# SwiGLU output products of three chunks in the seven-product form, with the gated rows as operands

## The chip, the cores and the metric

One core of one Trainium2 chip runs the whole step. The metric is the device time of one execution in microseconds; the kernel before has three runs, and the changed kernel is timed beside it.

## What is computed

One layer of a hybrid decoder on 544 tokens (512 of a prompt, 32 of eight sampled sequences), width 1024, float32. What the change touches is the feed-forward block, which stands in the layer twice, ahead of the token mixing and behind it:

```python
def swiglu(h, w_in, w_out):
    a, b = jnp.split(h @ w_in, 2, axis=-1)
    return (jax.nn.silu(a) * b) @ w_out

def run(x, ...):
    for l in range(DEPTH):
        x = x + 0.5 * swiglu(rmsnorm(x, norm_ffn1[l]), ffn1_w_in[l], ffn1_w_out[l])
        m, k, v, lf, s_fin = token_mix(rmsnorm(x, norm_mix[l]), w_in_mix[l], ...)
        x = x + m
        x = x + 0.5 * swiglu(rmsnorm(x, norm_ffn2[l]), ffn2_w_in[l], ffn2_w_out[l])
    return rmsnorm(x, norm_final), ...
```

`w_in` is 1024 by 5632, `w_out` is 2816 by 1024. The token mixing (projections, a gated linear recurrence and two forms of attention) is not touched.

## The kernel before, in words

Everything is kept with features on the 128 partitions and the 544 tokens in the free dimension, in two halves of 272. A float32 product is made of three passes: each operand is split into a rounded high part (`_hi`) and the rest (`_lo`), and high·high, high·low and low·high are summed in PSUM. ScalarE writes the high parts (a copy to float32r), VectorE the low parts (a subtraction).

The 2816 gate columns are 22 tiles of 128, worked in chunks of 4, 6, 6 and 6 (`CHUNKS`, L40). A chunk first makes its gate tiles (silu of one column tile times another), one **unit** for each, and then multiplies these rows into all 1024 output columns in four **out units** of 256 columns each, which are added to the residual `xT`. Units are numbered through the whole program; unit u uses weight slot u % 2, so that while TensorE works on one unit, ScalarE and VectorE split the weights of the next, and SyncE loads those of the one behind.

Chunk 0 and all out units are plain products (`products`, L2262): 3 passes for each tile of 128 rows, 128 columns and 272 tokens. Chunks 1 to 3 make their gate tiles by a seven-product form of a 2 by 2 block product (`seven_products`, L2391): the weights of a tile pair are four blocks of 128 by 512, `block_sums` and its relations (L2928 to L2971) form the sums `S1` to `S4` of them and the low parts, and the activations stand ready as seven operands `B11 ... T4`. So seven block products of 12 matmuls each take the place of eight. They go to five PSUM banks (`Z_BANKS`, L244), and VectorE joins them in five steps of 272 columns (L3008, L3013, L3018, L3022, L3026), with two bank copies (`z_kept`) by ScalarE (L2628, L2630). Then come the silu (L2607, L2635), the gated product (`z_gated`, L2973) and the split of the gated rows (`z_gated_hi`, L2609, and `z_gated_lo`, L2980).

There is no scheduler: each engine's order is written out in these functions, and an engine takes its instructions strictly in that order. VectorE's order for one gate unit is `seven_products_vector` (L2987): between the five steps of this unit stand the weight sums and the low parts of the next one. The out units are drained by `add_out` (L3028), two instructions of 544 columns that read PSUM and add half of it to `xT`. TensorE may begin a product only when its bank has been read; these waits are the `z_silu`, `z_step`, `z_copied` and `drained` waits at L2405 to L2440, and `g_wait` (L2461) holds an out unit until the gated rows are split. The slot waits of the loads are in `slot_free` (L2135).

The lines that the order of work hangs on, of a gate unit on VectorE:

```python
                if blocks:
                    block_sum_four(nxt, z + 1)
                    block_lo_gate(nxt, z + 1)
                else:
                    split_lo(nxt // 2, nxt % 2, last_kt)
                dve.wait_ge(z_product, 6 * z + 3)
                dve.wait_ge(z_copied, 2 * z + 1)
                nc.vector.tensor_tensor(z_part[:, 0, :], z_kept[:, 0, :], bank(beta), ALU.subtract).then_inc(z_step, 1)
                if blocks:
                    block_lo_sums(nxt, z + 1)
```

## Time and profile before

| | |
|---|---|
| median of 3 runs | 1224.8 us (1224.14 to 1225.08) |
| the profiled execution | 1225.52 us, of which its span is 1223.6 us |
| mean granted TensorE clock | 0.998 |
| TensorE, VectorE, ScalarE, GpSimdE busy | 98%, 72%, 48%, 8% of the span |
| DMA | 177.38 MB, 145 GB/s on average |

The span is what the trace shows of one execution. Busy shares are averages over stages: the two feed-forward blocks fill most of the span, the mixing the middle of it. A line number belongs to the kernel before. In a timeline the columns are the start, the duration, the engine, the line and the operation; in the table of windows they are the stretch and its length, each engine's busy time and number of instructions, the granted clock, and the DMA share and rate.

### The profile page before, as it was taken

How to read it: one execution, taken by the hardware profiler on the slowest of the kernel's cores; microseconds unless marked ns; L12 is line 12 of the kernel's file. 1: busy time of each engine (PE TensorE's matmuls, PEld its weight loads, DVE VectorE, ACT ScalarE, POOL GpSimd, SP SyncE). 2: the span in 40 equal slices, each digit the busy share in tenths (PEclk: the TensorE clock that was granted, in tenths of full speed). 3: DMA queues.
4: the chain of work that ended last, by engine and by line, in shares of the span. 5: the costliest groups of instructions: out<-in, count | busy, mean ns of one | idle time of the engine just before them, and what ended most of it. 6: DMA issues, size and time to landing. Idle time of an engine off the chain costs nothing.

```text
span 1223.6 us, 29870 instructions
## 1 busy us (share of the span) xinstructions
PE 1194.9 (98%) x11909; PEld 1115.8 (91%) x11909; DVE 882.9 (72%) x1661; ACT 586.7 (48%) x1101; POOL 102.4 (8%) x247
## 2 busy tenths in 40 slices
PE   9999999999999999998989999999999999999998
PEld 8999999999999999996656666699999999999998
DVE  6889848847959899746775676654889748838944
ACT  6354424524534344526867776634254424414534
POOL 1000000000013000000412522123000000000000
PEclk9999999999999999999999999999999999999999
DMA  8133333223334454376899997723133333233322
GB/s 212 53 87 103 113 95 101 89 89 103 96 100 153 129 132 104 104 241 201 307 351 351 367 363 247 254 78 97 53 91 102 110 95 104 87 102 88 96 78 74
DMA packets 195633, 177.38 MB, mean 145 GB/s; under 512 B 11921, under 2 KB 157874, under 8 KB 195250
## 3 DMA queue, kind: packets, MB, share of 16 engines
q1 hardware_dynamic: 194338, 171.93, 44.8%
q0 software_dynamic: 1104, 3.67, 0.8%
q8 instruction: 88, 1.44, 0.5%
q14 instruction: 39, 0.32, 0.1%
q10 hardware_dynamic: 64, 0.02, 0.0%
HBM read 164.42 MB, written 11.16 MB: 143 GB/s over the span
## 4 chain that ended last, share of the span: by engine, by line
PE 90%; DVE 3%; ACT 2%; issue 2%; DMA 2%; POOL 1%; ACTq 0%; DVEq 0%; POOLq 0%
PE ps L2400 38%; PE ps L2262 37%; PE ps L1071 2%; PE ps L1156 2%; PE ps L2492 2%; PE ps L1171 2%; PE ps L996 1%; PE ps L1036 1%; PE ps L1016 1%; DMA s_states<-in_state_hgrn 1%; DMA out<-s_states 1%; ACT d_keysT L1416 1%; PE ps L834 1%; PE ps L2508 0%; DMA gain_rows<-in_norm_final 0%
## 5 line engine op out<-in xcount | busy, mean ns | idle before, releaser
L2400 PE MATMUL ps<-b_lo,z_hi 128*128 128x272 f32 x1232 | 357.3, 290 | 0.0
L2400 PE MATMUL ps<-b_hi,z_lo 128*128 128x272 f32 x1008 | 290.6, 288 | 0.0
L2400 PE MATMUL ps<-b_hi,z_hi 128*128 128x272 f32 x1008 | 290.2, 288 | 0.0
L2400 PEld LDWEIGHTS ps<-b_lo,z_hi 128*128 128x128 f32 x1232 | 231.3, 188 | 0.0
L2400 PEld LDWEIGHTS ps<-b_hi,z_hi 128*128 128x128 f32 x1008 | 190.1, 189 | 0.0
L2400 PEld LDWEIGHTS ps<-b_hi,z_lo 128*128 128x128 f32 x1008 | 189.8, 188 | 0.0
L2557 ACT ACTIVATE w_hi<-w_raw 128x1536 fp32r<-128x1536 f32 (+2 forms) x48 | 74.7, 1556 | 161.8 <-PE ps L2262 161.8
L2262 PE MATMUL ps<-g_hi,w_hi 128*128 128x272 f32 x704 | 148.0, 289 | 0.3 <-DVE g_lo L2901 0.3
L2262 PE MATMUL ps<-g_lo,w_hi 128*128 128x272 f32 x704 | 147.5, 288 | 0.0
L2262 PE MATMUL ps<-g_hi,w_lo 128*128 128x272 f32 x704 | 146.8, 287 | 0.0
L3033 DVE SCALAR_TENSOR_TENSOR xT<-ps,xT 128x544 f32<-128x544 f32 x70 | 47.4, 719 | 97.9 <-PE ps L2262 97.9
L2956 DVE TENSOR_TENSOR z_lo<-z_sum,z_hi 128x1024 fp32r<-128x1024 f32 x132 | 113.6, 864 | 0.0
L2262 PEld LDWEIGHTS ps<-g_hi,w_hi 128*128 128x128 f32 x704 | 110.9, 188 | 0.8 <-DVE g_lo L2901 0.8
L2262 PEld LDWEIGHTS ps<-g_lo,w_hi 128*128 128x128 f32 x704 | 111.5, 189 | 0.0
L2262 PEld LDWEIGHTS ps<-g_hi,w_lo 128*128 128x128 f32 x704 | 111.2, 188 | 0.0
L2851 DVE TENSOR_TENSOR w_lo<-w_raw,w_hi 128x1536 fp32r<-128x1536 f32 (+2 forms) x47 | 89.7, 1908 | 15.2 <-ACT w_hi L2557 14.9
L2635 ACT ACTIVATE z_gate<-z_gate 128x272 f32<-128x272 f32 x36 | 15.5, 432 | 163.7 <-DVE z_gate L3026 163.7
L2956 DVE TENSOR_TENSOR z_lo<-w_raw,z_hi 128x1024 fp32r<-128x1024 f32 x88 | 83.8, 953 | 0.0
L1416 ACT ACTIVATE d_keysT<-ps 128x512 f32<-128x512 f32 x100 | 55.6, 594 | 52.4 <-PE ps L1071 52.1
L2585 ACT ACTIVATE z_hi<-w_raw 128x1024 fp32r<-128x1024 f32 x44 | 46.5, 1056 | 60.4 <-PE ps L2262 56.7
L1156 PE MATMUL ps<-d_keysT,d_queries 128*32 128x256 f32 x512 | 69.1, 389 | 1.4 <-issue 1.4
L2933 DVE TENSOR_TENSOR z_sum<-w_raw 128x1024 f32<-128x1024 f32 x44 | 53.8, 1223 | 22.0 <-PE ps L2400 17.7
(441 smaller groups left out, 2441.4 us busy)
## 6 DMA issues: line engine op xcount, KB each, us to landing
w_raw<-in_ffn_w_in SPq DMA_DIRECT2D x87, 512.0 KB, 5.0
d_keys<-in_cache_k SPq DMA_DIRECT2D x128, 256.0 KB, 5.3
...
w_raw<-in_w_in_mix SPq DMA_DIRECT2D x28, 512.0 KB, 4.8
...
w_raw<-in_w_out_mix SPq DMA_DIRECT2D x8, 512.0 KB, 4.6
...
```

Source lines behind the costliest of these rows:

```text
L1071: mm = pe.transpose(ps[:, B_KT + r, (k * SET_PAGES + m) * HP:(k * SET_PAGES + m + 1) * HP], d_k[n % K_RING][rows, m, j * P:(j + 1) * P], i ...
L1156: mm = pe.matmul(ps[g * NR:(g + 1) * NR, B_S, pp * 2 * PAGE:(pp + 1) * 2 * PAGE], d_q[b % 2][:, j * NR:(j + 1) * NR], keys, start=(j == 0) ...
L1171: pe.matmul(out, d_pT[b % 2][:, half, k, q * NR:(q + 1) * NR], src[:, q, :], start=(k == 0), stop=(k == 3), skip_group_check=True).then_in ...
L1416: nc.scalar.activation(d_kT[:, x % 2, k, :], ps[:, B_KT + k, :], ACT.Copy).then_inc(kc_act, 1)
L2262: mm = pe.matmul(bank(4 * j + 2 * t + half), wp, xp[:, k, half * HALF:(half + 1) * HALF], start=(k == 0 and wp is w[0] and xp is x_hi), st ...
L2400: mm = pe.matmul(bank(out), w[j][:, a, k * P:(k + 1) * P], x, start=(k == 0 and n_pass == 0 and not more), stop=(k == KB - 1 and n_pass == ...
L2557: nc.scalar.activation(w_hi[j][:, 0:kt * UC], w_raw[j][:, 0:kt * UC], ACT.Copy).then_inc(w_hi_ready, 1)
L2585: nc.scalar.activation(z_hi[j][:, A11:A12 + 1, :], z_raw[j][:, 0:2, :], ACT.Copy).then_inc(z_his, 1)
L2851: nc.vector.tensor_tensor(w_lo[j][:, 0:kt * UC], w_raw[j][:, 0:kt * UC], w_hi[j][:, 0:kt * UC].bitcast(F32), ALU.subtract).then_inc(w_lo_r ...
L2933: nc.vector.tensor_tensor(z_sum[j][:, S3:S1 + 1, :], z_raw[j][:, 0:4:3, :], z_raw[j][:, 2:3, :].to_broadcast([P, 2, BLOCK]), ALU.add).then ...
L2956: return nc.vector.tensor_tensor(z_lo[j][:, out, :], src, z_hi[j][:, out, :].bitcast(F32), ALU.subtract)
L3033: op = nc.vector.scalar_tensor_tensor(x, unit_psum(j, t), weight, x, ALU.mult, ALU.add)
```

## The change

The 22 gate tiles are worked in chunks of 4, 4, 4, 4 and 6. In chunks 1 to 3 (`BLOCKED`) the output product too is made by the seven-product form. The four gated tiles and the two token halves are the four blocks of one operand: the tiles 0 and 1 give `B11` and its neighbour, the tiles 2 and 3 give `B21` and `B22`. VectorE makes `T2`, `U1`, `T3` and `T4` of them, and seven operands are split in high and low, where four tiles were. They lie in rows of `g_full`, `g_high` and `g_low`. Such a chunk has two out units instead of four, each with 512 output columns: one load of weight blocks serves two results (v = 0 and 1), each a set of seven products of 6 matmuls. VectorE joins each result in the same five steps and adds it to `xT` in three instructions (`out_added`). A gated tile is no longer split by itself in these chunks. Chunk 0 and the last chunk keep the plain output product, and the counters of semaphores are renumbered.

```diff
 D_FF = 2816
 KD = D // P
 KF = D_FF // P
-CHUNKS = (4, 6, 6, 6)
+CHUNKS = (4, 4, 4, 4, 6)
+BLOCKED = (1, 2, 3)
...
+        g_full = [at(f"g{f + 1}_blocks", [P, 12, 2, HALF], F32, Z0 + 28 * (1 - f) * ROW) for f in range(2)]
+        g_low = [at(f"g{f + 1}_blocks_lo", [P, 6, 2, HALF], F32R, Z0 + 28 * (1 - f) * ROW) for f in range(2)]
+        g_high = [at(f"g{f + 1}_blocks_hi", [P, 6, 2, HALF], F32R, Z0 + (28 * (1 - f) + 6) * ROW) for f in range(2)]
...
+            def load_out_blocks(pair, j, w, k0):
+                slot_free(pair, j)
+                for r in range(2):
+                    dst = w_raw[j][:, r * 2 * BLOCK:(r + 1) * 2 * BLOCK].rearrange("p (k c) -> p k c", c=UC)
+                    src = w[0, k0 * P:(k0 + 4) * P, (2 * j + r) * UC:(2 * j + r + 1) * UC]
+                    sp.dma_start(dst, src.rearrange("(k p) n -> p k n", p=P)).then_inc(w_landed[j], 16)
...
+            def out_products(unit_n, j, z, f, c):
+                y = Y_AT[z]
+                def part(v, which, a, b, more=False):
+                    return product(j, Z_BANKS[v][which], a, (v, 2 + v), g_part_hi(f, b), g_part_lo(f, b), more)
+                def operand(b):
+                    if j == 0:
+                        pe.wait_ge(g_ready, g_from(f, c, G_LO) + TURN_ORDER.index(b) + 1)
+                pe.wait_ge(z_los, 4 * z + 2)
+                pe.wait_ge(w_lo_ready, unit_n)
+                pe.wait_ge(z_silu, 2 * (y - 1))
+                operand(B11)
+                part(0, 0, A11, B11).then_inc(z_product, 1)
+                pe.wait_ge(z_step, 5 * (y - 1))
+                operand(U1)
+                part(0, 1, S1, U1).then_inc(z_product, 1)
+                pe.wait_ge(z_silu, 2 * y)
+                part(1, 0, A11, B11).then_inc(z_product, 1)
+                pe.wait_ge(z_step, 5 * y)
+                part(1, 1, S1, U1).then_inc(z_product, 1)
+                pe.wait_ge(z_los, 4 * z + 3)
+                operand(T2)
+                part(0, 2, S2, T2).then_inc(z_product, 1)
+                operand(T3)
+                part(0, 3, S3, T3).then_inc(z_product, 1)
+                pe.wait_ge(z_los, 4 * z + 4)
+                operand(T4)
+                part(0, 4, A22, T4).then_inc(z_product, 1)
+                pe.wait_ge(w_lo_ready, unit_n + 1)
+                pe.wait_ge(z_copied, 2 * y + 2)
+                operand(B22)
+                part(0, 1, S4, B22, more=True).then_inc(z_product, 1)
+                operand(B21)
+                part(0, 0, A12, B21, more=True).then_inc(z_product, 1)
+                part(1, 2, S2, T2).then_inc(z_product, 1)
+                pe.wait_ge(z_step, 5 * y + 1)
+                part(1, 3, S3, T3).then_inc(z_product, 1)
+                pe.wait_ge(z_step, 5 * y + 2)
+                part(1, 4, A22, T4).then_inc(z_product, 1)
+                pe.wait_ge(z_copied, 2 * y + 4)
+                part(1, 1, S4, B22, more=True).then_inc(z_product, 1)
+                part(1, 0, A12, B21, more=True).then_inc(mm_done, 1)
...
+            def g_parts_hi(f, c, ns, gated):
+                act.wait_ge(gated_ready, g_from(f, c, GATED) + gated)
+                for n in ns:
+                    nc.scalar.activation(g_part_hi(f, n), g_part(f, T2 if n == U1 else n), ACT.Copy).then_inc(ghi_ready, 1)
+            def keep(y, bank_n, which, products):
+                act.wait_ge(z_product, products)
+                nc.scalar.activation(z_kept[:, which, :], bank(bank_n), ACT.Copy).then_inc(z_copied, 1)
...
+            def out_products_scalar(unit_n, z, f, c):
+                y, done = Y_AT[z], PRODUCTS_AT[z]
+                if unit_n % 2 == 0:
+                    z_silu_first(unit_n - 1, z - 1)
+                    g_parts_hi(f, c, TURN_ORDER[2:], 11)
+                act.wait_ge(z_step, 5 * (y - 1) + 3)
+                keep(y, Z_BANKS[0][0], 0, done + 1)
+                keep(y, Z_BANKS[0][1], 1, done + 2)
+                block_hi_raw(unit_n + 1, z + 1)
+                block_hi_raw_up(unit_n + 1, z + 1)
+                block_hi_sums(unit_n + 1, z + 1)
+                block_hi_last(unit_n + 1, z + 1)
+                act.wait_ge(z_step, 5 * y + 3)
+                keep(y + 1, Z_BANKS[1][0], 0, done + 3)
+                keep(y + 1, Z_BANKS[1][1], 1, done + 4)
...
+            def gated_place(f, c, tile):
+                if c not in BLOCKED:
+                    return z_up[:, :, :]
+                k = tile % 2
+                return g_full[f][:, B11:G_B12 + 1:G_B12 - B11, k, :] if tile < 2 else g_full[f][:, B21:B22 + 1, k, :]
+            def g_first_sum(f, c):
+                dve.wait_ge(gated_ready, g_from(f, c, GATED) + 2)
+                nc.vector.tensor_tensor(g_part(f, T2), g_part(f, B11), g_full[f][:, G_B12, :, :], ALU.subtract)\
+                    .then_inc(gated_ready, 1)
+            def g_sums(f, c, k):
+                done = g_from(f, c, GATED) + (4, 8)[k]
+                t2, b22 = g_part(f, T2)[:, k, :], g_part(f, B22)[:, k, :]
+                dve.wait_ge(gated_ready, done)
+                nc.vector.tensor_tensor(t2, t2, b22, ALU.add).then_inc(gated_ready, 1)
+                nc.vector.tensor_tensor(g_part(f, T3)[:, k, :], b22, g_full[f][:, G_B12, k, :], ALU.subtract)\
+                    .then_inc(gated_ready, 1)
+                dve.wait_ge(gated_ready, done + 1)
+                nc.vector.tensor_tensor(g_part(f, T4)[:, k, :], t2, g_part(f, B21)[:, k, :], ALU.subtract)\
+                    .then_inc(gated_ready, 1)
+            def g_parts_lo(f, c, ns):
+                for n in ns:
+                    dve.wait_ge(ghi_ready, g_from(f, c, G_HI) + TURN_ORDER.index(n) + 1)
+                    nc.vector.tensor_tensor(g_part_lo(f, n), g_part(f, T2 if n == U1 else n),
+                                            g_part_hi(f, n).bitcast(F32), ALU.subtract).then_inc(g_ready, 1)
...
+            def out_added(unit_n, y, v):
+                j = unit_n % 2
+                lower, upper = halves(xT[:, 4 * j + 2 + v, :]), halves(xT[:, 4 * j + v, :])
+                dve.wait_ge(z_step, 5 * y + 5)
+                nc.vector.scalar_tensor_tensor(lower, z_up[:, :, :], 0.5, lower, ALU.mult, ALU.add)
+                nc.vector.scalar_tensor_tensor(upper[:, 1, :], z_gate[:, 1, :], -0.5, upper[:, 1, :], ALU.mult, ALU.add)
+                if v:
+                    dve.wait_ge(mm_done, unit_n + 1)
+                nc.vector.scalar_tensor_tensor(upper[:, 0, :], bank(Z_BANKS[v][0]), -0.5, upper[:, 0, :], ALU.mult, ALU.add)\
+                    .then_inc(z_silu, 2)
+                if v:
+                    dve.wait_ge(z_silu, 2 * y + 2)
+                    dve.sem_inc(drained, 1)
+            def out_products_vector(unit_n, z, f, c, before):
+                y, done = Y_AT[z], PRODUCTS_AT[z]
+                nxt = unit_n + 1
+                before()
+                block_sums(nxt, z + 1)
+                block_sum_two(nxt, z + 1)
+                block_sum_four(nxt, z + 1)
+                block_lo_gate(nxt, z + 1)
+                alpha, gamma, beta, delta, eps = Z_BANKS[0]
+                first_part(y, beta, done + 5)
+                second_part(y, delta, done + 6)
+                lower_right(y)
+                block_lo_sums(nxt, z + 1)
+                lower_left(y, eps, done + 7)
+                upper_right(y, gamma, done + 8)
+                block_lo_two(nxt, z + 1)
+                dve.wait_ge(z_product, done + 9)
+                out_added(unit_n, y, 0)
+                block_lo_up(nxt, z + 1)
+                alpha, gamma, beta, delta, eps = Z_BANKS[1]
+                first_part(y + 1, beta, done + 10)
+                second_part(y + 1, delta, done + 11)
+                lower_right(y + 1)
+                lower_left(y + 1, eps, done + 12)
+                block_lo_four(nxt, z + 1)
+                upper_right(y + 1, gamma, done + 13)
...
+                        if c in BLOCKED:
+                            p0 += pairs
+                            def g_last(c=c, z=z0 + kt):
+                                z_gated(z - 1, gated_place(f, c, 3))
+                                g_sums(f, c, 1)
+                                g_parts_lo(f, c, TURN_ORDER[2:])
+                            out_products_vector(2 * p0, z0 + kt, f, c, g_last)
+                            out_products_vector(2 * p0 + 1, z0 + kt + 1, f, c,
+                                                lambda: out_added(2 * p0, Y_AT[z0 + kt] + 1, 1))
+                            def before(unit_n=2 * p0 + 1, y=Y_AT[z0 + kt + 1] + 1):
+                                out_added(unit_n, y, 1)
+                            p0 += 1
+                            continue
```

The helpers `first_part`, `second_part`, `lower_right`, `lower_left` and `upper_right` are the five steps that stood in `seven_products_vector`, and `keep` is the bank copy of ScalarE. In a gate unit of a blocked chunk `z_gated_lo` is gone; the third one has `g_first_sum` and the low parts of `B11` and `U1`, the fourth `g_sums`.

**VectorE behind the last gate tile of chunk 1 and in its first out units, before** (`z_gate`, `z_part`, `z_up`, `z_kept` are parts of a result, `g_hi` and `g_lo` the high and low part of a gated tile, `w_raw`, `w_hi` and `w_lo` those of weights):

```order
L3026 TENSOR_TENSOR z_gate<-z_part,ps 128x272 [waits z_product]
L2978 TENSOR_TENSOR z_up<-z_gate,z_up 128x544 [waits z_silu,z_step]
L2984 SCALAR_TENSOR_TENSOR g_lo<-z_up,g_hi 128x544 [waits ghi_ready]
L2851 TENSOR_TENSOR w_lo_85<-w_raw_81,w_hi_83 128x1536 [waits w_hi_ready]
L3033 SCALAR_TENSOR_TENSOR xT<-ps,xT 128x544 [waits mm_done]
L3033 SCALAR_TENSOR_TENSOR xT<-ps,xT 128x544
L2851 TENSOR_TENSOR w_lo_84<-w_raw_80,w_hi_82 128x1536 [waits w_hi_ready]
L3033 SCALAR_TENSOR_TENSOR xT<-ps,xT 128x544 [waits mm_done]
L3033 SCALAR_TENSOR_TENSOR xT<-ps,xT 128x544
```

**The same engine behind the last gate tile of chunk 1, now** (`g_blocks` holds the seven operands, `g_block` the last of them; `z_sum`, `z_hi` and `z_lo` are sums, high and low parts of weight blocks):

```order
L3180 TENSOR_TENSOR z_gate<-z_part,ps 128x272 [waits z_product]
L3118 TENSOR_TENSOR g_blocks<-z_gate,z_up 128x2x272 [waits z_silu,z_step]
L3145 TENSOR_TENSOR g_blocks<-g_blocks 128x272 [waits gated_ready]
L3146 TENSOR_TENSOR g_blocks<-g_blocks 128x272
L3149 TENSOR_TENSOR g_block_128<-g_blocks 128x272 [waits gated_ready]
L3156 TENSOR_TENSOR g_blocks_lo<-g_blocks,g_blocks_hi 128x544 [waits ghi_ready] x2
L3156 TENSOR_TENSOR g_block_lo<-g_block_128,g_block_hi 128x544 [waits ghi_ready]
L3156 TENSOR_TENSOR g_blocks_lo<-g_blocks,g_blocks_hi 128x544 [waits ghi_ready] x2
L3072 TENSOR_TENSOR z_sum_91<-w_raw_81 128x1024 [waits mm_done,w_landed1]
L3078 TENSOR_TENSOR z_sum_91<-w_raw_81,z_sum_91 128x512 [waits z_sums]
L3084 TENSOR_TENSOR z_sum_91<-w_raw_81,z_sum_91 128x512 [waits z_sums]
L3095 TENSOR_TENSOR z_lo_89<-w_raw_81,z_hi_87 128x1024 [waits z_his]
```

Between the last gate tile and the drain of the first out unit stood a gated product, one low part and a weight split. Now there are the gated product, three sums, five low parts and the whole set of weight sums, and the first joining step comes behind all of these.

**VectorE in the first out unit of chunk 1, further on, now:**

```order
L3095 TENSOR_TENSOR z_lo_89<-z_sum_91,z_hi_87 128x512 [waits z_his]
L3228 SCALAR_TENSOR_TENSOR xT<-z_up,xT 128x544 [waits z_step,z_product]
L3229 SCALAR_TENSOR_TENSOR xT<-z_gate,xT 128x272
L3232 SCALAR_TENSOR_TENSOR xT<-ps,xT 128x272
L3095 TENSOR_TENSOR z_lo_89<-w_raw_81,z_hi_87 128x512 [waits z_his]
L3162 TENSOR_TENSOR z_part<-z_kept,ps 128x272 [waits z_copied,z_product]
L3167 TENSOR_TENSOR z_part<-z_part,ps 128x272 [waits z_step,z_product]
L3172 TENSOR_TENSOR z_up<-z_part,z_kept 128x272 [waits z_step,z_copied]
L3176 TENSOR_TENSOR z_up<-z_part,ps 128x272 [waits z_product]
L3095 TENSOR_TENSOR z_lo_89<-z_sum_91,z_hi_87 128x512 [waits w_hi_ready]
L3180 TENSOR_TENSOR z_gate<-z_part,ps 128x272 [waits z_product]
L3228 SCALAR_TENSOR_TENSOR xT<-z_up,xT 128x544 [waits z_step]
```

Before, an out unit was two drains and a weight split. Now the three additions of the first result stand in front of the five steps of the second result, and the additions of the second behind those.

## Rows read from the trace of the kernel before

**Rows 1.** The page: busy time of two engines, and TensorE's granted clock in 40 slices
```profile
PE 1194.9 (98%) x11909; PEld 1115.8 (91%) x11909; DVE 882.9 (72%) x1661; ACT 586.7 (48%) x1101; POOL 102.4 (8%) x247
PEclk9999999999999999999999999999999999999999
```
**Rows 2.** The chain that ended last, chunks 1 and 2: start, length, what
```profile
89.70 63.57 PE ps L2400 x504
153.27 36.07 PE ps L2262 x288
189.34 63.57 PE ps L2400 x504
252.91 36.07 PE ps L2262 x288
```
**Rows 3.** Windows: one gate unit of chunk 2
```profile
210.53:221.12 10.59, 10.59 (x87) 10.59 (x86) 9.61 (x15) 5.51 (x10) 0.00 (x0) 1.00 0.37 101
```
**Rows 4.** Timeline of VectorE, the same kind of unit
```profile
200.05 1.23 DVE L2933 TENSOR_TENSOR z_sum<-w_raw 128x1024 f32<-128x1024 f32 x1 [0.97 <-PE ps L2400]
201.20 0.72 DVE L2978 TENSOR_TENSOR z_up<-z_gate,z_up 128x544 f32<-128x544 f32 x1
201.83 0.69 DVE L2939 TENSOR_TENSOR z_sum<-w_raw,z_sum 128x512 f32<-128x512 f32 x1
202.64 0.72 DVE L2984 SCALAR_TENSOR_TENSOR g_lo<-z_up,g_hi 128x544 fp32r<-128x544 f32 x1
203.28 0.68 DVE L2945 TENSOR_TENSOR z_sum<-w_raw,z_sum 128x512 f32<-128x512 f32 x1
203.88 1.22 DVE L2956 TENSOR_TENSOR z_lo<-w_raw,z_hi 128x1024 fp32r<-128x1024 f32 x1
205.02 0.43 DVE L3008 TENSOR_TENSOR z_part<-z_kept,ps 128x272 f32<-128x272 f32 x1
205.37 1.22 DVE L2956 TENSOR_TENSOR z_lo<-z_sum,z_hi 128x1024 fp32r<-128x1024 f32 x1
206.50 0.43 DVE L3013 TENSOR_TENSOR z_part<-z_part,ps 128x272 f32<-128x272 f32 x1
...
209.35 0.43 DVE L3026 TENSOR_TENSOR z_gate<-z_part,ps 128x272 f32<-128x272 f32 x1
```
**Rows 5.** Timeline of ScalarE, the same unit
```profile
201.95 0.66 ACT L2612 ACTIVATE g_hi<-z_up 128x544 fp32r<-128x544 f32 x1 [0.61 <-DVE z_up L2978]
202.51 0.62 ACT L2589 ACTIVATE z_hi<-w_raw 128x512 fp32r<-128x512 f32 x1
203.03 0.38 ACT L2628 ACTIVATE z_kept<-ps 128x272 f32<-128x272 f32 x1
203.31 0.39 ACT L2630 ACTIVATE z_kept<-ps 128x272 f32<-128x272 f32 x1
```
**Rows 6.** Timeline, two engines, behind the fifth gate tile of chunk 2
```profile
242.36 0.40 ACT L2607 ACTIVATE z_gate<-ps 128x272 f32<-128x272 f32 x1 [0.32 <-PE ps L2400]
...
242.93 0.72 DVE L2978 TENSOR_TENSOR z_up<-z_gate,z_up 128x544 f32<-128x544 f32 x1 [1.36 <-ACT z_gate L2607]
```
**Rows 7.** Timeline: TensorE held by a low part of VectorE, first out unit
```profile
69.10 0.73 DVE L2901 TENSOR_TENSOR g_lo<-ffn_gated,g_hi 128x544 fp32r<-128x544 f32 x1 [0.72 <-ACT g_hi L2578]
...
69.89 0.52 PE L2262 MATMUL ps<-g_hi,w_hi 128*128 128x272 f32 x2 [0.17 <-DVE g_lo L2901]
```
**Rows 8.** Windows at the head of the mixing, behind the last projection
```profile
553.00:556.00 3.00, 1.38 (x47) 0.94 (x49) 3.00 (x4) 2.00 (x5) 2.43 (x7) 1.00 0.56 168
556.00:560.00 4.00, 4.00 (x102) 2.86 (x88) 1.13 (x7) 2.34 (x4) 0.00 (x0) 0.57 0.88 268
560.00:564.00 4.00, 4.00 (x95) 2.47 (x82) 3.70 (x18) 1.98 (x4) 0.00 (x0) 1.00 0.27 77
```
**Rows 9.** The page: loads of gate weights, KB each, us from issue to landing
```profile
w_raw<-in_ffn_w_in SPq DMA_DIRECT2D x87, 512.0 KB, 5.0
```

265 lines of the change are left out of this document (163 added, 102 removed).

## The prediction

> **What bounds the kernel now.** I began with the page's first line [rows 1]: TensorE is busy 98% of the span and its granted clock never leaves the upper level, 2.4 GHz. A busy TensorE can still be a waiting one, so I took the chain of waits next [rows 2]: chunk 1 is one piece of 504 matmuls in 63.57 us and one of 288 in 36.07 us, and chunk 2 follows without a gap. That is 126.1 ns for a matmul of a seven-product unit and 125.2 ns for one of a plain out unit, with nothing between them. TensorE is the only bound in the feed-forward blocks, and a matmul left out there is worth its full 126 ns as long as nothing else comes to hold it.
>
> The next question is how near the second engine is. In one gate unit of 10.59 us VectorE is busy 9.61 us [rows 3]. The 72% of the page is an average over stages; here it is 91%, and the timeline shows the rest as one wait of 0.97 us at the unit's head [rows 4]. ScalarE, at 5.51 us, is far from its limit.
>
> **The change part by part.** *TensorE.* A tile of gated rows costs 288 / 6 = 48 matmuls in the plain out units. Twelve tiles of a feed-forward block move to the new form: 576 matmuls of 125.2 ns, 72.1 us, go; three chunks with 2 x 84 = 168 matmuls of 126.1 ns, 63.6 us, come. The gate units are as many as before. That saves 8.6 us a block, **17.1 us** in all, if TensorE never waits. Smaller groups (6 matmuls instead of 12) cost nothing by themselves, since the pitch is that of single matmuls.
>
> *VectorE.* From one start to the next in the timeline, 272 columns take 0.35 us, 512 take 0.60, 544 take 0.635 and 1024 take 1.14 [rows 4]. The weight sums and low parts of a unit are three instructions of 1024 and five of 512, 6.4 us; the five joining steps are 1.75. The new shapes (three additions of 544, 272 and 272 to `xT`, sums of 272, low parts of 544) are in no row. I bound them by the pitch, 0.35 and 0.635, and by the full duration of one instruction, 0.43 and 0.72 [rows 4], and take the pitch, since the nearest rows have the same operands and follow each other so. A blocked chunk then holds six weight sets (38.4), four times five steps in the gate units and four times five in the out units (14.0), four gated products (2.5), a sum of 544 and six of 272 (2.7), seven low parts (4.4), and four times three additions of 1.34 (5.3): **67.4 us of VectorE in a chunk of 6 x 10.6 = 63.6 us of TensorE**. The gate units have room (8.8 us of 10.6 without `z_gated_lo`), the two out units have 13 to 16 us of work in 10.6 each, and since only one unit is prepared ahead, room in one place does not help in the other.
>
> *Where TensorE waits.* I follow the order of the change through the two out units, counting from the first one's start; TensorE's products are 6 x 0.126 = 0.76 us each.
> - The gated product of tile 3 needs ScalarE's two silus. In the row it starts 0.6 us behind the unit [rows 6]; here VectorE, which has 10.7 us of work in the third gate unit and 9.9 in the fourth, ends its last step only at 0.1, and the second silu comes behind that, so 0.9. Then the gated product and three sums end at 2.8. ScalarE writes five high parts at 0.56 each [rows 5] from 2.85, VectorE the low parts from 3.55 at 0.635. Low part `T2` is done at 4.3; TensorE has made its four products of `B11` and `U1` by 3.0 and waits **1.3**. The later operands keep ahead of it.
> - VectorE is through with the low parts at 6.7, then come the four instructions of the next unit's sums, to 10.4, and only then `first_part`, done at 10.9. TensorE's eleventh product writes the bank which that step reads, and could start at 8.85: **2.1**, and 0.15 for the late bank copies.
> - TensorE ends the unit at 14.1. The next one starts in the bank of the first result. Its last addition stands behind `block_lo_sums`, two steps and `block_lo_two`, and is done at 15.7: **1.6**.
> - After two products it wants the bank of the second result, and the order there is `block_lo_up`, five steps, `block_lo_four` in between, and three additions: 20.35 instead of 17.2, **3.15**.
> - From there TensorE has 12 products, 9.1 us, and VectorE keeps up. The unit ends at 29.4 instead of 21.2. The next gate unit starts with VectorE 3 us late; its waits reach back to what is done by then, and VectorE gains 1.8 us in a unit, so nothing more is lost.
>
> This is 8.3 us a blocked chunk, six times: 49.6 us. An instruction that waits for two semaphores starts up to 0.1 later than one with a single wait (0.17 in [rows 6] against 0.03 from product to high part in [rows 4, 5]); the steps that follow each other directly pay it, 0.25 us a chunk on the path, 1.5 in all. TensorE itself restarts 0.06 behind its releaser [rows 7], which is in the above. Moved otherwise, and free: the loads. Two per out unit of 512 KB land in 5.0 us [rows 9], with a whole unit of time behind the issue; if VectorE is late, they are issued late by as much, but then VectorE is what is waited for. ScalarE's seven high parts for four (3 x 0.56 a chunk) are covered by its idle half.
>
> *The clock.* One place of the trace shows it falling. At the head of the mixing TensorE was busy 1.38 of 3 us, and in the 4 us behind that the mean granted clock was 0.57, before it was 1.00 again [rows 8]: (1 - 0.57) / 0.5 of 4 us are some 3.4 us at the lower level, 1.2 GHz, worth 1.7 us. The Trainium skill (TensorE: Matmul & The Clock Gate, Part 1) says that the slow clock is the default and activity is what releases it; by this rule the change could pay for its waits a second time, and the trace agrees. The second out unit has such a place: from 14.1 to 20.35 TensorE works 1.5 of 6.3 us. I take a fall in three of the six chunks, 3 x 1.7 = 5 us; none and all six are the bounds, 0 and 10.
>
> **Sum.** 1225.5 - 17.1 + 49.6 + 1.5 + 5 = 1264.5 us against the profiled execution, which lies 0.7 us above the median: **1264 us**.
>
> **Rivals.** *The saving arrives (faster).* VectorE stays hidden, and the time is 1225 - 17 = 1208. The Trainium skill (Perfetto Trace Analysis, Identifying the Most-Contended Engine) says to improve the engine with the highest occupancy, and that is TensorE, from whose list the change strikes 144 matmuls. By that rule alone it is 1208. For it: two chunks in a row without a wait of TensorE [rows 2]. Against it: 67.4 us of VectorE do not fit in 63.6, whatever their order. It decides where the waits of a chunk stay under 17.1 / 6 = 2.85 us; the two out units would have to lose 5 us of VectorE work. Chance 0.05.
>
> *Only the surplus counts.* The order leaks less than I walked, and TensorE loses just 67.4 - 63.6 = 3.8 us a chunk: 1225 - 17 + 23 = 1231. Against it: four different products wait at four places, and the work in front of each is fixed by the order. Chance 0.10.
>
> *The clock falls everywhere or the new instructions take their full duration.* The first gives 1269. By the second some 28 new instructions of a chunk cost 0.085 more, 2.4 us and 14 in all, if all lie on the path: 1273 to 1278. Chance 0.15.
>
> **Numbers.** The forecast has 0.70, with 1255 to 1270 as its own range (hand-offs of 0.02 to 0.08 us, clock 0 to 10). To hold eight in ten of all cases the range reaches a little into both neighbours: 1246 to 1277. A measurement of this kernel tells 0.2%, 2.5 us, from no change. Faster 0.05, same 0.02, slower 0.93.
>
> **What would show it.** In the trace after, TensorE's waits should stand in the lines of the products with `g_hi` operands, 8 us a blocked chunk at four or five places, the longest near 3 us and released by an addition to `xT`; gate units should still take 10.6 us, a blocked chunk 71 to 74 us, and the last chunk be unchanged. A granted clock below 1 in second out units shows the last term. I am wrong if the out units take 10.6 us each (then 1208), if VectorE has idle time of more than 2 us in them while TensorE waits (then a wait on ScalarE or a load is what I missed), or if gate units grow.

## The result, and the profile after

| | before | after |
|---|---|---|
| median of the runs | 1224.8 us | 1272.8 us (1270.6 to 1274.8, 3 runs) |
| ratio | | 1.0388 [1.0363, 1.0413]: slower |
| profiled execution, span | 1225.5, 1223.6 us | 1270.6, 1268.7 us |
| mean granted clock | 0.998 | 0.986 |

The forecast was 1264 us with a range of 1246 to 1277. The page of after, the lines that answer to [rows 1] and [rows 9], and its chain:

```profile
PE 1197.7 (94%) x11765; PEld 1112.2 (88%) x11765; DVE 1017.3 (80%) x1961; ACT 631.1 (50%) x1211; POOL 102.1 (8%) x247
PEclk9999999998999999999999999999999998999999
...
PE 65%; DVE 23%; issue 7%; ACT 3%; DMA 1%; POOL 1%; DVEq 0%; ACTq 0%; POOLq 0%
...
w_raw<-in_ffn_w_out SPq DMA_DIRECT2D x24, 512.0 KB, 4.4
```

The 144 matmuls are gone (11909 - 11765), yet TensorE's busy time has not shrunk: matmuls are longer at the lower clock and behind a wait (0.36 to 0.39 us instead of 0.29 for the first one, in the rows below). A quarter of the chain is now VectorE (23%). The new loads land in 4.4 us and are waited for nowhere.

TensorE's waits, the list of after (engine, instruction held, releaser, then us in total, times, longest); before, no seven-product matmul waited for VectorE:

```profile
PE ps L2441 <- DVE xT L3232: 22.0, 10, 3.0
PE ps L2441 <- DVE z_part L3162: 10.6, 6, 1.8
PE ps L2441 <- DVE g_blocks_lo L3156: 8.3, 6, 1.8
```

TensorE's timeline in chunk 2 (start, duration, instruction, and in brackets the idle time before it):

```profile
210.65 0.36 PE L2441 MATMUL ps<-g_blocks_hi,z_hi 128*128 128x272 f32 x1 [1.08 <-DVE g_blocks_lo L3156]
...
217.18 0.39 PE L2441 MATMUL ps<-g_blocks_hi,z_hi 128*128 128x272 f32 x1 [1.76 <-DVE z_part L3162]
...
226.82 0.39 PE L2441 MATMUL ps<-g_blocks_hi,z_hi 128*128 128x272 f32 x1 [2.96 <-DVE xT L3232]
```

These three are the low part of `T2`, `first_part` before the eleventh product, and the second result's addition to `xT`, in the order of the walk. The fourth, at the start of the second out unit, is only 0.3 to 0.4 us here, since the clock had fallen at 218.4 and TensorE was late itself. By the starts of the matmuls in chunk 3 of the second block, where it did not fall before the last of them, the four are 1.25, 1.93, 1.54 and 3.12 us, where the walk had 1.3, 2.1, 1.6 and 3.15. In the first chunk of each block the first wait is longer, 2.0 us, with 0.6 more ahead of it.

VectorE is the other half of the picture. Windows of after: the four gate units of chunk 2, then one whole blocked chunk, from the first product of its out units to that of the next chunk's (columns as in [rows 3]: PE, PEld, DVE, ACT, POOL, the clock, the DMA share and rate):

```profile
157.30:167.90 10.60, 10.60 (x86) 10.60 (x85) 9.86 (x20) 3.26 (x7) 0.00 (x0) 1.00 0.04 11
167.90:178.50 10.60, 10.60 (x86) 10.60 (x85) 10.41 (x18) 4.30 (x8) 0.00 (x0) 1.00 0.43 118
178.50:189.00 10.50, 10.50 (x86) 10.50 (x85) 10.04 (x16) 4.47 (x9) 0.00 (x0) 1.00 0.55 173
189.00:199.40 10.40, 10.40 (x85) 10.40 (x84) 10.40 (x19) 6.74 (x15) 0.00 (x0) 1.00 0.20 58
206.38:278.59 72.21, 66.26 (x506) 65.22 (x505) 69.24 (x118) 33.34 (x61) 0.00 (x0) 0.98 0.30 88
```

TensorE is never idle in the gate units, but VectorE is busy there for 9.9 to 10.4 us of 10.6 too, and for 69.2 of the 72.2 us of the chunk.

**Where the time went.** The feed-forward blocks hold six blocked chunks. From the first to the last matmul with `g_blocks` operands, the two out units take 32.5, 29.6, 31.4, 32.8, 31.1 and 31.0 us: 188.4, against 6 x 21.2 = 127.1 without waits. Less the 17.1 saved, that is +44.2. The mixing adds 1.1: it begins behind a last run of plain products that has moved by 21.2 us (401.73 to 422.89), and before the second block the like has moved by 22.3 (852.89 to 875.16). Together 45.3, where the span has grown by 45.1 us. The mixing's 1.1 need not be a price of the change: this stretch is the same in all kernels here and lasts between 449.2 and 457.8 us in their profiled executions, 451.0 before.

Of the 188.4, 6.4 belong to the clock: the same six intervals take 182.0 us in the kernel with fillers below, where the clock does not fall in them. The gate units behind them give 1.4 back, so the two blocks as wholes differ by 5.0 us. The clock fell at eight places of the feed-forward blocks, five times behind the longest wait of a chunk and three times behind the wait of the eleventh product; one of the five:

```profile
299.70:304.00 4.30, 4.30 (x24) 4.30 (x24) 3.86 (x5) 2.10 (x3) 0.00 (x0) 0.60 0.72 201
```

### The profile page after: what moved, and what is told of

Read it like the earlier page. It is cut to its first block, busy times and chain, and to the rows that moved or that the text cites. A ratio compares the mean times of both kernels' runs of the same rounds, so it can differ in the third digit from the quotient of the medians.

```text
span 1268.7 us, 30008 instructions
## 1 busy us (share of the span) xinstructions
PE 1197.7 (94%) x11765; PEld 1112.2 (88%) x11765; DVE 1017.3 (80%) x1961; ACT 631.1 (50%) x1211; POOL 102.1 (8%) x247
## 4 chain that ended last, share of the span: by engine, by line
PE 65%; DVE 23%; issue 7%; ACT 3%; DMA 1%; POOL 1%; DVEq 0%; ACTq 0%; POOLq 0%
PE ps L2441 27%; PE ps L2309 23%; DVE z_lo L3095 6%; PE ps L1104 2%; PE ps L1189 2%; PE ps L2593 2%; DVE z_sum L3072 2%; DVE g_blocks_lo L3156 2%; PE ps L1204 2%; PE ps L1029 1%; DVE z_sum L3078 1%; DVE g_blocks L3118 1%; DVE z_part L3167 1%; DVE z_up L3172 1%; PE ps L1069 1%
## 5 line engine op out<-in xcount | busy, mean ns | idle before, releaser
L3095 DVE TENSOR_TENSOR z_lo<-z_sum,z_hi 128x1024 fp32r<-128x1024 f32 x168 | 144.5, 861 | 0.0
L2441 PE MATMUL ps<-g_blocks_hi,z_hi 128*128 128x272 f32 x288 | 90.7, 315 | 42.3 <-DVE xT L3232 22.0
L2658 ACT ACTIVATE w_hi<-w_raw 128x2048 fp32r<-128x2048 f32 (+2 forms) x32 | 50.9, 1591 | 104.7 <-PE ps L2309 104.7
L2441 PEld LDWEIGHTS ps<-g_blocks_hi,z_hi 128*128 128x128 f32 x288 | 59.0, 205 | 48.3 <-DVE xT L3232 19.1
L2441 PE MATMUL ps<-g_blocks_lo,z_hi 128*128 128x272 f32 x288 | 87.7, 304 | 0.0
L2441 PE MATMUL ps<-g_blocks_hi,z_lo 128*128 128x272 f32 x288 | 87.7, 304 | 0.0
L2724 ACT ACTIVATE z_kept<-ps 128x272 f32<-128x272 f32 x120 | 42.0, 390 | 66.0 <-DVE z_up L3172 56.1
L2990 DVE TENSOR_TENSOR w_lo<-w_raw,w_hi 128x2048 fp32r<-128x2048 f32 (+2 forms) x31 | 61.6, 1986 | 13.4 <-ACT w_hi L2658 13.1
L1189 PE MATMUL ps<-d_keysT,d_queries 128*32 128x256 f32 x512 | 69.4, 391 | 0.0
L2309 PE MATMUL ps<-g_hi,w_hi 128*128 128x272 f32 x320 | 68.5, 289 | 0.3 <-DVE g_lo L3040 0.3
L2309 PE MATMUL ps<-g_lo,w_hi 128*128 128x272 f32 x320 | 68.1, 288 | 0.0
```

The source lines that it names most:

```text
L1189: mm = pe.matmul(ps[g * NR:(g + 1) * NR, B_S, pp * 2 * PAGE:(pp + 1) * 2 * PAGE], d_q[b % 2][:, j * NR:(j + 1) * NR], keys, start=(j == 0) ...
L2309: mm = pe.matmul(bank(4 * j + 2 * t + half), wp, xp[:, k, half * HALF:(half + 1) * HALF], start=(k == 0 and wp is w[0] and xp is x_hi), st ...
L2441: mm = pe.matmul(bank(out), w[j][:, a, column * P:(column + 1) * P], x[:, k, :], start=(k == 0 and n_pass == 0 and not more), stop=(k == l ...
L2658: nc.scalar.activation(w_hi[j][:, 0:kt * UC], w_raw[j][:, 0:kt * UC], ACT.Copy).then_inc(w_hi_ready, 1)
L2724: nc.scalar.activation(z_kept[:, which, :], bank(bank_n), ACT.Copy).then_inc(z_copied, 1)
L2990: nc.vector.tensor_tensor(w_lo[j][:, 0:kt * UC], w_raw[j][:, 0:kt * UC], w_hi[j][:, 0:kt * UC].bitcast(F32), ALU.subtract).then_inc(w_lo_r ...
```

## The experiments

The theory on record was that four products of a blocked chunk wait for VectorE, which has more to do in the two out units than TensorE, and that the clock's falls come on top. The rivals were that the small chunks cost by themselves, that lateness builds up over chunks, that one wait in one order is to blame, and, later, that the whole list of VectorE is the bound and no place in it. Each kernel is compared with the kernel before on the same chip (1223.5, 1225.0, 1225.6 and 1224.5 us in the four lots, in order: 1 to 4, 5 to 8, 9 and 10, 11 and 12).

### 1. The chunks alone

```diff
-BLOCKED = (1, 2, 3)
+BLOCKED = ()
...
```

> Chunks of 4, 4, 4, 4 and 6, all output products plain. If the seven-product output form is what costs time, this is the kernel before again: the same matmuls (22 tiles of 48 in each block), one more change from gate to out units, 1224.8 us within 2. If the smaller chunks themselves cost something (rival: more changes of stage, less room ahead of the out units), a good part of the 48 us is seen here.

Measured 1227.0 us, ratio 1.0029 [1.0015, 1.0043]. No seven-product matmul is on TensorE's list of waits, and the plain chunks start 66.4 us apart. Of the 1.4 us that its span is longer, 0.75 stand in the mixing, where the clock fell twice. The form costs the time, not the chunks.

### 2. One blocked chunk of three

```diff
-BLOCKED = (1, 2, 3)
+BLOCKED = (3,)
...
```

> Only chunk 3 has the seven-product output form; chunks 1 and 2 have plain out units. If each blocked chunk costs its own share (its waits, 7 to 9 us, and about one fall of the clock, 1.7 us, against 2.85 us of matmuls saved), two chunks instead of six cost a third of 48 us: 1241, between 1237 and 1244. If the loss builds up from chunk to chunk (rival: VectorE's lateness is carried on), it is clearly less than a third, under 1236.

Measured 1242.8 us, ratio 1.0146 [1.0129, 1.0163]: 18 us for two blocked chunks, 9 each, where the change has 48 / 6 = 8. Its out units take 31.1 and 31.0 us, as in the change. The trace puts it closer: the two feed-forward blocks are 7.2 and 7.0 us longer than before, against 7.1 and 7.6 a blocked chunk in the change, and the mixing, which is unchanged, happened to take 6.8 us more in this execution. So each chunk pays its own price, and nothing builds up.

### 3. Matmuls in the waits

```diff
+            def fill(n, b=4):
+                for _ in range(n):
+                    pe.matmul(ps[:, b, 0:P], ones[:, :], ones[:, :], start=True, stop=True)
...
+                if j:
+                    pe.wait_ge(z_step, 5 * (y - 1))
+                    fill(5)
...
+                if j:
+                    fill(12)
...
+                if j == 0:
+                    fill(4)
...
+                if j == 0:
+                    fill(7, 6)
```

> The changed kernel with matmuls of ones (4, 7, 5 and 12 of 128 columns, about 0.23 us each) placed ahead of the four long waits of each blocked chunk, so that TensorE stays active in them. If the clock falls because of the waits, and costs what the trace of the changed kernel shows (8 falls in the two blocks, 1.7 us each), this gives 1272.8 - 13 = about 1260, with a granted clock near 0.998. If the waits alone are the cost and the low clock falls into time that is waited anyway (rival), the time stays at 1271 to 1274 though the clock is full; if the fillers outlast the waits it is slower.

Measured 1264.2 us, ratio 1.0332 [1.0317, 1.0346]; clock 1.0. That is 0.0056 or 7 us less than the change (less than I expected). In the profiled executions 5.0 us of it lie in the feed-forward blocks, and that is the price of the clock there; the rest lies in the mixing, where the clock fell twice in the change and not here. The out units take 182.0 us in all. A chunk of it, windows:

```profile
205.41:277.91 72.50, 71.31 (x562) 70.11 (x561) 69.38 (x119) 33.50 (x61) 0.00 (x0) 1.00 0.30 88
```

With TensorE busy for 71.3 us the chunk still lasts 72.5, and VectorE's busy time is unchanged. The chunk of the change above, 72.21 us, is not shorter: counted on VectorE, from the gated product of tile 3 to that of the next chunk, it is 72.48 us in the change (207.16 to 279.64) and 72.50 here, with the same 118 instructions at the same distances.

### 4. The joining steps ahead of the weight sums

In the first out unit `first_part`, `second_part` and `lower_right` stand before the sums of the next weights, so that the eleventh product is not held.

```diff
                 before()
...
+                if unit_n % 2 == 0:
+                    first_steps()
                 block_sums(nxt, z + 1)
...
```

> In the first out unit VectorE makes the first three joining steps ahead of the weight sums of the next unit. The wait of 1.9 us ahead of TensorE's eleventh product loses its releaser. If each wait is worth its own length (rival), six times 1.9 us go: 1261. If VectorE's whole list of the chunk sets the time, the order inside it doesn't matter: the wait ahead of the eleventh product is gone, those ahead of the bank copies and at the second out unit's start grow by as much, and the time is 1272.8 within 3.

Measured 1273.6 us, ratio 1.0409 [1.0391, 1.0426]: nothing gained. The wait for `z_part` left the list, and its time came back under two others (compare the list of after):

```profile
PE ps L2441 <- DVE xT L3232: 27.5, 12, 3.0
PE ps L2441 <- ACT z_kept L2724: 5.8, 4, 1.5
```

### 5. Less work in the out units

On the kernel with fillers (4, 7, 2 and 8 of them) the first two of the three additions of each result to `xT` are left out.

```diff
-                nc.vector.scalar_tensor_tensor(lower, z_up[:, :, :], 0.5, lower, ALU.mult, ALU.add)
-                nc.vector.scalar_tensor_tensor(upper[:, 1, :], z_gate[:, 1, :], -0.5, upper[:, 1, :], ALU.mult, ALU.add)
```

> On the kernel with filled waits (1264.2 us, full clock; fillers cut to 4, 7, 2 and 8). Left out: the first two of the three additions of each result to xT in the blocked chunks, so three quarters of their output never reach the residual. That takes 1.0 us of VectorE four times a chunk. If VectorE's list sets the time of a blocked chunk, 2 us a chunk go at least (two of the four stand ahead of the last long wait), up to 3.9 if all four count: 1240 to 1252. If the waits are set by the hand-offs between the engines and not by its load (rival), less than 1 us a chunk: above 1258.

Measured 1253.6 us, ratio 1.0240 [1.0222, 1.0257]: 11 us or 1.9 a chunk less than with all additions. Windows of one chunk:

```profile
203.21:273.27 70.06, 69.37 (x548) 68.51 (x547) 65.62 (x110) 33.72 (x62) 0.00 (x0) 1.00 0.31 91
```

VectorE lost 3.8 us of busy time and the chunk 2.4. (The two blocks are 14.2 us shorter, 2.4 a chunk; the ratio shows less, since the mixing took 4.1 us more in this execution.) TensorE, with its fillers, is busy for 69.4 of 70.1 us here and so nearly full itself. So the run bounds the gain from below.

### 6 and 7. One more low part, in a gate unit or in an out unit

The prediction said that the gate units have room which is of no use to the out units. If so, an extra instruction of 1024 columns is free in the one and not in the other. Both write a low part a second time, on the kernel with fillers.

```diff
+                    if c in BLOCKED and n == 1:
+                        block_lo_again(nxt, z + 1)
```

> On the kernel with filled waits (1264.2): one instruction of 1024 elements (a low part written twice) more for VectorE in the second gate unit of each blocked chunk, 1.14 us, six in all. As the prediction has it, VectorE gains 1.8 us in such a unit and room there is of no use elsewhere: 1264 to 1266. If instead VectorE's list of the whole chunk, gate units too, sets its length (rival), about 1.0 us a chunk: 1270 to 1271.

```diff
                 block_sum_two(nxt, z + 1)
+                if unit_n % 2 == 0:
+                    block_lo_again(nxt, z + 1)
```

> On the kernel with filled waits (1264.2): the same instruction more in the first out unit of each blocked chunk instead. Both theories have it on the path, 1.14 us six times: 1271. If it is hidden (hand-offs set the waits), 1264 to 1265.

Measured 1269.1 us, ratio 1.0360 [1.0345, 1.0375], and 1269.5 us, ratio 1.0366 [1.0350, 1.0383]. One chunk of each, windows, the gate unit's first:

```profile
208.96:282.48 73.52, 71.57 (x563) 70.15 (x561) 70.44 (x120) 33.47 (x61) 0.00 (x0) 1.00 0.30 87
```

and the out unit's:

```profile
206.47:279.98 73.51, 71.30 (x562) 70.10 (x561) 70.43 (x120) 33.56 (x61) 0.00 (x0) 1.00 0.29 87
```

The chunk is 1.0 us longer in both, 73.52 and 73.51 against 72.50, for 1.05 us more of VectorE. It makes no difference where the instruction stands. (The ratios say 0.6 to 0.7 us a chunk with some 0.4 of uncertainty; the traces, 1.0 in every chunk. It is not the 1.14 of a pitch, since at either place the instruction parts two sums of which the second takes the first's result, which saves 0.12.) There is no room in the gate units that is not already used.

### 8. The sums S2 and S4 on GpSimd

In the blocked chunks GpSimd makes the two additions of 512 columns of each weight set. In the second out unit TensorE makes the upper products first, so that the bank of the second result is wanted late, ScalarE copies the banks before the last high parts, and 8 fillers a chunk stay.

```diff
+                    nc.gpsimd.tensor_tensor(z_sum[j][:, S2, :], z_raw[j][:, 0, :], z_sum[j][:, S1, :], ALU.add).then_inc(z_sums, 1)
...
+                    nc.gpsimd.tensor_tensor(z_sum[j][:, S4, :], z_raw[j][:, 1, :], z_sum[j][:, S2, :], ALU.add).then_inc(z_sums, 1)
```

> A try for a faster version, with filled waits: in the blocked chunks GpSimd makes the two weight sums of 512 (some 2.1 us each, by its row of 544 elements), TensorE finishes the first result of the second out unit before it begins the second, and ScalarE makes the bank copies of the second result ahead of the last high parts. If VectorE's load is the bound, 1.2 us a unit leave its list and a blocked chunk goes from 72.5 to about 69 us: 1264 - 20 = 1244, still above the kernel before. If GpSimd's reads slow VectorE or its sums come late (rival), it is 1255 or more.

Measured 1279.0 us, ratio 1.0450 [1.0431, 1.0469]: the slowest of all, 35 us over what I expected. Windows of a chunk:

```profile
206.84:282.76 75.92, 70.20 (x522) 68.66 (x521) 72.84 (x110) 33.69 (x61) 20.54 (x12) 0.96 0.29 84
```

Two groups of instructions on each engine, VectorE's of 146 us with chunks 2 and 3, GpSimd's of the whole span (shapes, count, then busy us, mean ns of one, and idle time before):

```profile
L3135 DVE TENSOR_TENSOR z_lo<-z_sum,z_hi 128x1024 fp32r<-128x1024 f32 x12 | 20.4, 1701 | 0.0
L3135 DVE TENSOR_TENSOR z_lo<-w_raw,z_hi 128x1024 fp32r<-128x1024 f32 x12 | 19.9, 1662 | 0.3
...
L3656 POOL TENSOR_TENSOR z_sum<-w_raw,z_sum 128x512 f32<-128x512 f32 x36 | 66.6, 1850 | 463.0 <-DVE z_sum L3112 463.0
L3658 POOL TENSOR_TENSOR z_sum<-w_raw,z_sum 128x512 f32<-128x512 f32 x36 | 57.4, 1595 | 2.8
```

VectorE has twelve sums less and is busy for 72.8 us instead of 69.4. Its waits in this chunk are for ScalarE, 0.9 and 0.7 us, as without GpSimd; it waits nowhere for a sum that comes late. Its low parts of 1024 columns take 1.7 us on average, where they take 1.22 in [rows 4]. The timeline of both engines shows one of them:

```profile
220.18 2.31 DVE L3135 TENSOR_TENSOR z_lo<-z_sum,z_hi 128x1024 fp32r<-128x1024 f32 x1
...
217.76 2.20 POOL L3656 TENSOR_TENSOR z_sum<-w_raw,z_sum 128x512 f32<-128x512 f32 x1 [14.51 <-DVE z_sum L3112]
220.04 1.37 POOL L3658 TENSOR_TENSOR z_sum<-w_raw,z_sum 128x512 f32<-128x512 f32 x1
```

GpSimd started at 220.04, VectorE at 220.18; GpSimd ended at 221.41, VectorE 1.08 us after that, near the 1.22 that such an instruction takes alone. The first GpSimd instruction was long in the same way, behind a low part of VectorE that ended at 218.82. They go one after the other. VectorE's joining steps that read PSUM, at 218.74 and 219.27, took their usual 0.43 and 0.44 us beside the same GpSimd instruction. The Trainium skill (SBUF — State Buffer, SBUF: two separate sides) says that the two engines share a pair of ports, that whichever starts first holds it for its whole instruction, when VectorE reads two inputs from SBUF, and that the other is blocked. The trace agrees: 2.31 us is 1.23 of blocking and one low part.

### 9. The same kernel without the work of the sums

```diff
-                    nc.gpsimd.tensor_tensor(z_sum[j][:, S2, :], z_raw[j][:, 0, :], z_sum[j][:, S1, :], ALU.add).then_inc(z_sums, 1)
+                    nc.gpsimd.tensor_tensor(z_sum[j][:, S2, 0:16], z_raw[j][:, 0, 0:16], z_sum[j][:, S1, 0:16], ALU.add).then_inc(z_sums, 1)
```

> The kernel with the sums on GpSimd, but GpSimd's two additions a unit in the blocked chunks are made over 16 of their 512 columns alone, and the parts of S2 and S4 are taken of the raw blocks A11 and A12 (the second products of the blocked chunks are then not the reference's). All waits, the order of the products and the order of the VectorE steps stay as in the kernel with the sums on GpSimd, which took 1279.0 us. Theory 1 (GpSimd and VectorE slow each other: in that kernel the 1024-column low parts took 1.66 to 1.70 us where they take 1.22 alone, and GpSimd's 512-column additions 1.60 to 1.85): VectorE's list of a blocked chunk is 67.4 - 8 x 0.69 = 61.9 us, under TensorE's 63.6 and its 2.7 of fillers, and the chunks fall from some 75.5 us to 67 to 69: 1228 to 1240 us. Theory 2 (the loss lies in the waits and in the order of the products, or in the high parts that come after the copies on ScalarE): at most 10 us are gained, 1268 us or more.

Measured 1243.2 us, ratio 1.0151 [1.0132, 1.0171]; a chunk, window:

```profile
200.82:270.12 69.30, 67.00 (x522) 65.73 (x521) 62.53 (x106) 33.57 (x61) 7.75 (x12) 1.00 0.32 92
```

37 us come back, so the loss of kernel 8 was the work on GpSimd and not its order: theory 1, though 3 us above its range. VectorE's list has the same shapes in the same order as in kernel 8, and it is busy for 62.5 us instead of 72.8: 10.3 us of a chunk were stretch. (A part of the 37 is the clock, which fell six times in the blocks of kernel 8 and never in those of this one; by kernel 3 that is a few us.) The expectation counts 8 sums in a chunk; there are twelve, two for each of six weight sets. The chunk is now 6.8 us longer than VectorE's busy time. Something else begins to hold it: VectorE waits for TensorE for 2.3 us of this chunk, which it did not do in kernel 8.

### 10. The order of kernel 8, all sums on VectorE

```diff
+                if j:
...
+                    part(0, 0, A12, B21, more=True).then_inc(z_product, 1)
+                    pe.wait_ge(z_silu, 2 * y)
+                    part(1, 0, A11, B11).then_inc(z_product, 1)
```

> The kernel with the sums on GpSimd, but with all sums back on VectorE, at the places that they have in the change: what stays of it is the order of TensorE's products in the second out unit (the upper half first, so that the bank of the second result is wanted late), the copies of the banks ahead of the last high parts, and 8 filler matmuls a chunk. Theory 1 (a blocked chunk lasts as long as VectorE's list of 67.4 us and some 5 us in which VectorE waits, whatever TensorE's order): near the kernel with fillers alone (1264 us), 1258 to 1268 us. Theory 2 (the places of the waits decide, and this order hides two of the three of the second out unit, 3.1 and 1.5 us a chunk less 1 of filler): 1242 to 1252 us. Theory 3 (this order is what cost the kernel with the sums on GpSimd its time): 1275 us or more.

Measured 1265.8 us, ratio 1.0326 [1.0310, 1.0343]. A chunk (window), and under it TensorE's waits in the span:

```profile
205.13:277.62 72.49, 67.24 (x523) 65.75 (x521) 69.37 (x119) 33.48 (x61) 0.00 (x0) 1.00 0.30 88
```
```profile
PE ps L2441 <- DVE z_part L3202: 16.8, 12, 1.8
PE ps L2441 <- DVE xT L3272: 8.9, 10, 1.4
PE ps L2441 <- DVE g_blocks_lo L3196: 4.5, 6, 1.1
```

This is the run that decides. The waits stand at other products, with other lengths, 20 fewer filler matmuls run, and the chunk is 72.49 us against 72.50. VectorE's chain, with its waits for ScalarE, gives this number. I summed it from its timeline in this chunk: the start-to-start times of its 118 instructions by shape (0.35, 0.60, 0.635 and 1.14, as in [rows 4]; the windows count 119, with one that lies across an edge) make 67.6 us; waits for ScalarE, at the gated product of tile 3 and at the low part behind it, make 1.8; and the rest is 3.1. Of this, 2.5 is in pairs where an instruction waits for the VectorE instruction just before it, nearly always for its result, and 0.5 in the two sums that come right behind the last addition of a result to `xT`, where `drained` is raised. The same sum in kernel 3, and in chunk 2 of the change itself, gives the same numbers. Such pairs in the timeline of after:

```profile
226.99 1.23 DVE L3072 TENSOR_TENSOR z_sum<-w_raw 128x1024 f32<-128x1024 f32 x1 [0.21 <-DVE xT L3232]
228.25 0.69 DVE L3078 TENSOR_TENSOR z_sum<-w_raw,z_sum 128x512 f32<-128x512 f32 x1
228.97 0.69 DVE L3084 TENSOR_TENSOR z_sum<-w_raw,z_sum 128x512 f32<-128x512 f32 x1
229.58 1.22 DVE L3095 TENSOR_TENSOR z_lo<-w_raw,z_hi 128x1024 fp32r<-128x1024 f32 x1
230.72 0.43 DVE L3162 TENSOR_TENSOR z_part<-z_kept,ps 128x272 f32<-128x272 f32 x1
231.25 0.44 DVE L3167 TENSOR_TENSOR z_part<-z_part,ps 128x272 f32<-128x272 f32 x1
231.79 0.44 DVE L3172 TENSOR_TENSOR z_up<-z_part,z_kept 128x272 f32<-128x272 f32 x1
```

From 230.72 to 231.25 it is 0.53 us, where the same step gives way to an independent one in 0.35 (205.02 to 205.37 in [rows 4]); a sum of 512 behind a sum takes 0.72 instead of 0.60. In the gate units most of these steps have other work between them; in the out units they stand together.

### 11. Dependent steps apart

```diff
                 first_part(y + 1, beta, done + 10)
+                block_lo_up(nxt, z + 1)
                 second_part(y + 1, delta, done + 11)
+                block_lo_four(nxt, z + 1)
                 lower_right(y + 1)
...
+                    block_lo_gate(nxt, z + 1)
                     block_sum_four(nxt, z + 1)
-                    block_lo_gate(nxt, z + 1)
```

> The kernel with the upper products first, and on VectorE no step straight behind the step whose result it takes, where another is at hand: the first low part between the sums, a sum or a low part between the joining steps. Nothing is left out. Theory 1 (VectorE's own chain is the whole chunk: in a blocked chunk of 72.49 us of that kernel, 67.6 us are the start-to-start times of its 119 instructions, 3.1 the extra 0.1 to 0.19 us of a step that waits for the VectorE instruction just before it, 1.8 waits for ScalarE): some 12 of those pairs go, 1.7 to 2 us a chunk, 10 to 12 us: 1253 to 1257 us. Theory 2 (the extra is hidden by something else that sets the end, a load or ScalarE): unchanged, 1263 us or more.

Measured 1261.8 us, ratio 1.0309 [1.0291, 1.0327]. Neither theory's number: the change to kernel 10 is 0.0017, 2 us, with the intervals overlapping, though the trace is plain (72.03 us a chunk instead of 72.49). By the same sum of VectorE's timeline most of the pairs are gone, 2.2 us, and new waits of 1.8 have come. VectorE's waits in one chunk:

```profile
DVE z_lo L3135 <- ACT z_hi L2738: 1.3, 2, 0.6
DVE g_blocks L3158 <- ACT z_gate L2746: 1.0, 1, 1.0
DVE g_blocks_lo L3196 <- ACT g_blocks_hi L2757: 0.7, 1, 0.7
```

The first line is new: the low part of `S2` was brought forward, and ScalarE's high part of it is not there yet. Most of the gain was given back to it.

### 12. Without the sums and without fillers

```diff
-                    fill(5)
...
-                fill(3)
...
                 first_part(y + 1, beta, done + 10)
+                block_lo_up(nxt, z + 1)
                 second_part(y + 1, delta, done + 11)
```

> The kernel with the sums left out (GpSimd's additions over 16 columns alone, the parts of S2 and S4 of the raw blocks, so the second products of the blocked chunks are not the reference's), without the 8 filler matmuls a chunk and with the joining steps of the out units apart from each other. It tells what the form is worth where VectorE has 6.9 us less in a chunk. Theory 1 (then TensorE is the bound, 63.6 us and 1 to 2.2 us of waits): chunks of 64.8 to 66 us against 66.4 before, 1216 to 1224 us, as fast as the kernel before or faster. Theory 2 (what the order costs TensorE stays, and the clock falls in its waits): 67 to 69 us a chunk, 1228 to 1240 us.

Measured 1247.1 us, ratio 1.0183 [1.0166, 1.0200]; a chunk (window), and under it TensorE's waits in the span:

```profile
201.57:271.64 70.07, 65.28 (x506) 63.82 (x505) 62.18 (x106) 33.80 (x61) 8.03 (x12) 1.00 0.32 91
```
```profile
PE ps L2441 <- DVE xT L3278: 12.0, 12, 1.0
PE ps L2441 <- ACT z_kept L2760: 8.4, 12, 1.0
PE ps L2441 <- DVE g_blocks_lo L3195: 6.5, 6, 1.1
```

Theory 1 fell, and even theory 2 was too hopeful. With 6.9 us less of VectorE work the form is still slower than the plain chunk of 66.4 us, and no engine is full: TensorE's list is 63.6 of 70.1, VectorE's busy time 62.2. Now they wait for each other, and for ScalarE's bank copies: in this chunk VectorE waits for TensorE for 2.7 us and for ScalarE for 4.2. (In the profiled execution the mixing took 4.6 us more than before; the blocks alone are 3.6 us a blocked chunk longer.) So behind the bound that the change meets stands a second one at about 69 to 70 us, a chain of hand-offs through three engines. Which link of it is the tightest stays open.

None of the twelve beats the kernel before. One with all its work would have to bring a blocked chunk from 72.5 to under 66.4 us, and the start-to-start times of VectorE alone are 67.6.

## Why the prediction was right, and where it was not

- **TensorE's saving**: 144 matmuls fewer, as counted; kernel 1 shows that nothing else of the regrouping costs more than 0.3%.
- **The waits of a blocked chunk**: 49.6 and 1.5 us were forecast, 51.1. At full clock (kernel 3) the two blocks are 39.0 us longer than before; with the 17.1 saved that makes 56.1. All four places are in the trace within 0.2 us of the walk, in its order, and the sign against them did not show: while TensorE waits in a chunk, VectorE is idle for 0.5 to 1.4 us, not for more than 2. Of the 5.0 us more, 2.7 are in the first chunk of each block. There the gated product of tile 3 starts 2.2 us behind the first product instead of 1.1, and the out units take 1.2 to 1.5 us longer; I take it that VectorE comes late out of the plain chunk, which no run tested. The rest is 0.4 us a chunk of hand-offs.
- **The term that was too small** is VectorE's list of 67.4 us with 0.25 for dependent steps. The pitches were right (its terms, unrounded, make 67.6, and so do the traces), the hand-offs are 3.1 us and the waits for ScalarE 1.8. The walk had the latter.
- **The clock**: 5 us forecast, from three falls of 1.7. The 5.0 measured agree by luck: there were eight falls in these blocks, and they cost less each. The three behind the eleventh product's wait cost nothing (a chunk with one such fall has VectorE's full-clock length, 72.48 us), since the slower matmuls lie in time that is waited anyway; the five behind the longest wait cost 0.9 to 1.0 us each (73.49 and 73.48 against 72.50). That [rows 1] shows the clock always at the upper level was a misreading: a digit there is a mean over some 31 us, and [rows 8] shows a fall inside one.
- **The mixing** was taken as unchanged and took 1.1 us more, no more than it varies by itself. So 1264.5 + 5.0 + 1.1 = 1270.6, which is the profiled execution; the median of the three is 2.2 us above it.
- **"The gate units have room ... room in one place does not help in the other"**: this sentence failed. The windows of after have VectorE busy for 9.9 to 10.4 us of each gate unit, and kernels 6 and 7 charge 1.0 us for the same instruction at either place. What room the gate units have goes into catching up with what the out units left over. VectorE works from one end of the chunk to the other, and the chunk lasts as long as its chain. The walk came out right because it followed that chain in its order; its waits are what TensorE shows of it. Kernels 4 and 10 moved them, and the chunk kept its length (72.50 us in the shortest of kernel 4, 72.48 in kernel 10, counted on VectorE).
- **Rival "the saving arrives"**, 1208: given 5%. Its condition, 5 us less of VectorE work, would not have been enough in the order of kernel 12, which has 6.9 less and is at 1.018. The rule of the Trainium skill (Perfetto Trace Analysis, Identifying the Most-Contended Engine), to improve the engine with the highest occupancy, named the engine that was the bound before, TensorE with 98% of the span. Followed alone it misled here, since the change pays for the 144 matmuls with VectorE's time: the kernel became 3.9% slower.
- **Rival "only the surplus counts"**, 1231: its mechanism, one full list against another, was nearer to the truth than I gave it credit for. Its price was wrong, since it compared pitches with pitches and left out 4.9 us a chunk of hand-offs and waits for ScalarE.
- **Rival "the clock falls everywhere or full durations"**: 1269 was its number for the clock, near the result by its size alone: a fall in each chunk did come, but cost 5.0 us in all and not 10. New instructions have the old pitch (an addition of 544 columns to `xT` is followed after 0.63 to 0.65 us), so the second half of it is out.
